# Stick-breaking attention with queries on partitions: suffix sums by a backwards scan on DVE

## The reference

```python
z = jnp.einsum('bqhd,bkhd->bhqk', qb, k).astype(jnp.float32) * scale
causal = key_pos[None, :] < t[:, None]
log_keep = jnp.where(causal, jax.nn.log_sigmoid(-z), 0.0)
suffix = lax.cumsum(log_keep, axis=3, reverse=True) - log_keep
attn = jnp.where(causal, jnp.exp(jax.nn.log_sigmoid(z) + suffix), 0.0)
return jnp.einsum('bhqk,bkhd->bqhd', attn, v.astype(jnp.float32)).astype(q.dtype)
```

## Time and profile before

| | |
|---|---|
| median of 3 runs | 2167.89 us (2167.81 to 2168.23) |
| the profiled execution: span from the first to the last instruction | 2165.9 us |
| PE busy with matmuls | 2142.8 us, 99% of the span |
| DVE busy | 1273.9 us, 59% |
| ACT busy | 784.7 us, 36% |
| PE's share of the chain that ended last | 95% |

### The profile page before, as it was taken

One profiled execution on the slowest core, in us unless ns is written; L12 is line 12 of the kernel. 1 busy time (PEld: TensorE's weight loads), 2 busy tenths in 40 slices (PEclk: granted clock), 3 DMA queues, 4 the chain that ended last, 5 costly groups with the idle time before them and its releaser, 6 DMA issues.

```text
span 2165.9 us, 24997 instructions
## 1 busy us (share of the span) xinstructions
PE 2142.8 (99%) x10363; PEld 1768.0 (82%) x10363; DVE 1273.9 (59%) x1673; ACT 784.7 (36%) x1044; POOL 26.6 (1%) x41
## 2 busy tenths in 40 slices
PE   7999999999999999999999999999999999999998
PEld 4888888888888887888888888888788888888887
DVE  6899897944665848435665554234843576555423
ACT  3323232323343354344343333135434435333312
POOL 1000000000000100000000000000000000000000
PEclk9999999999999999999999999999999999999999
DMA  9432232332232222312223232222232222323322
GB/s 316 145 117 83 97 103 83 99 115 98 98 102 98 98 79 78 131 64 92 84 86 110 82 113 97 88 77 88 78 124 71 85 91 80 113 81 111 103 88 78
DMA packets 181588, 217.86 MB, mean 101 GB/s; under 512 B 3932, under 2 KB 153188, under 8 KB 181220
## 3 DMA queue, kind: packets, MB, share of 16 engines
q1 hardware_dynamic: 178080, 209.47, 29.1%
q10 hardware_dynamic: 2948, 4.65, 0.6%
q0 software_dynamic: 448, 2.15, 0.3%
HBM read 212.06 MB, written 4.19 MB: 100 GB/s over the span
## 4 chain that ended last, share of the span: by engine, by line
PE 95%; DVE 2%; issue 1%; ACT 1%; DMA 0%; POOL 0%; SPq 0%; POOLq 0%; ACTq 0%; DVEq 0%
PE psum L1819 30%; PE psum L1821 30%; PE psum L1820 30%; PE psum L2234 1%; PE psum L2266 1%; DVE whl L518 1%; PE psum L1962 1%; PE psum L2246 1%; PE psum L2200 1%; DMA ada<-in_w_ada 0%; PE psum L2187 0%; PE psum L2219 0%; PE psum L1843 0%; POOL stat L682 0%; DVE hT L1502 0%
## 5 line engine op out<-in xcount | busy, mean ns | idle before, releaser
L1819 PE MATMUL psum<-hT,whl 128*128 128x512 f32 (+1 forms) x2064 | 789.4, 382 | 2.7 <-DVE whl L518 1.5
L1821 PE MATMUL psum<-hT,whl 128*128 128x512 f32 (+1 forms) x2064 | 783.3, 380 | 0.0
L1820 PE MATMUL psum<-hT,whl 128*128 128x512 f32 (+1 forms) x2064 | 783.1, 379 | 0.0
L518 DVE TENSOR_TENSOR whl<-raw,whl 128x1024 fp32r<-128x1024 f32 x361 | 438.5, 1217 | 429.2 <-ACT whl L511 428.9
L511 ACT ACTIVATE whl<-raw 128x1024 fp32r<-128x1024 f32 x361 | 376.7, 1047 | 421.5 <-PE psum L1821 387.1
L1819 PEld LDWEIGHTS psum<-hT,whl 128*128 128x128 f32 x2064 | 388.3, 188 | 84.2 <-issue 8.4
L1821 PEld LDWEIGHTS psum<-hT,whl 128*128 128x128 f32 x2064 | 388.3, 188 | 73.9
L1820 PEld LDWEIGHTS psum<-hT,whl 128*128 128x128 f32 x2064 | 388.4, 188 | 71.5 <-issue 0.2
L1819 PE MATMUL psum<-whl,ff 128*128 128x512 f32 x352 | 137.1, 390 | 0.0
L1821 PE MATMUL psum<-whl,ff 128*128 128x512 f32 x352 | 137.0, 389 | 0.0
L1820 PE MATMUL psum<-whl,ff 128*128 128x512 f32 x352 | 137.0, 389 | 0.0
(11 more groups left out here) (328 smaller groups left out, 2161.1 us busy)
## 6 DMA issues: line engine op xcount, KB each, us to landing
raw<-in_w_in SPq DMA_DIRECT2D x87, 1024.0 KB, 5.1
raw<-in_w_up SPq DMA_DIRECT2D x44, 1024.0 KB, 5.0
raw<-in_w_down SPq DMA_DIRECT2D x20, 1024.0 KB, 5.0
raw<-in_w_branch SPq DMA_DIRECT2D x12, 1024.0 KB, 5.1
raw<-in_w_out SPq DMA_DIRECT2D x12, 1024.0 KB, 5.0
ada<-in_w_ada SPq DMA_DIRECT2D x8, 1024.0 KB, 9.4
ada<-in_w_ada SPq DMA_DIRECT2D x8, 512.0 KB, 10.9
x<-in_x SPq DMA_DIRECT2D x4, 512.0 KB, 5.2
```

Source lines behind the costliest of these rows:

```text
L518: nc.vector.tensor_tensor(whl_view(w, 1), raw_view(w), whl_view(w, 0).bitcast(F), ALU.subtract).then_inc(w_lo, 1)
L1819: M(out_, stat_hi, mov_hi, start=start, stop=False, **kw)
L1820: M(out_, stat_hi, mov_lo, start=False, stop=False, **kw)
L1821: return M(out_, stat_lo, mov_hi, start=False, stop=stop, **kw)
```

## The change

Queries go on partitions and keys on columns, so that the sum over keys runs along the columns, and DVE does it by a scan.

- `sb_scores` exchanges the two operands, with the same segment widths, and adds the mask (eight `identb` times `sbaddb` matmuls) before it signals each head. The mask matrix is transposed.
- ACT's `sb_logs` stays. DVE's `sb_exponent(h)` at ph 1 and 2 takes the place of `sb_softplus` (ph 0, 1) and `sb_lo` (ph 2, 3): softplus, four scans that run backwards over a segment (`[:, ::-1]`), and z minus the running sum.
- ACT's `sb_exp` at ph 2 and 3 takes the exponential from SBUF to SBUF. PE's `sb_transposes(h)` at ph 4 and 5 takes the place of `sb_exponents`: ten 128x128 transposes to the head's banks. ACT's `sb_attnT` copies them to `sba`, and `sb_values` is as before.
- The split parts, `sbt`, `negtri`, `negones_r` and `sbmul` go, with their two copies on DVE at the start of the layers.

```diff
@@ ACT @@
-                def sb_hi(h):
-                    act.wait_ge(sp_ready, 2 * (4 * l + h) + 2)
-                    A(sphi[h % 2][:], sbs[h % 2][:], ACT.Copy).then_inc(sp_hi, 1)
-                    act.wait_ge(sp_sum, 4 * l + h + 1)
-                    A(sbt_hi[h % 2][:], sbt[h % 2][:], ACT.Copy).then_inc(sp_hi, 1)
-
                 def sb_exp(h):
+                    act.wait_ge(sb_e, 4 * l + h + 1)
+                    A(sbl[h % 2][:], sbs[h % 2][:], ACT.Exp).then_inc(sb_attn, 1)
+
+                def sb_attnT(h):
                     e = h % 2
-                    act.wait_ge(e_ps, 4 * l + h + 1)
+                    act.wait_ge(aT_ps, 4 * l + h + 1)
                     if h >= 2:
                         act.wait_ge(sbo_ps, 2 * l + h // 2)
-                    A(sba[e][:], psum[:, Z_BANK[e] * SEQ:Z_BANK[e] * SEQ + 1280], ACT.Exp).then_inc(sb_attn, 1)
+                    A(sba[e][:], psum[:, Z_BANK[e] * SEQ:Z_BANK[e] * SEQ + 1280], ACT.Copy).then_inc(aT_ready, 1)
...
-                        if ph in (1, 2):
-                            sb_hi(2 * p + ph - 1)
+                        if ph in (2, 3):
+                            sb_exp(2 * p + ph - 2)
                         if ph in (4, 5):
-                            sb_exp(2 * p + ph - 4)
+                            sb_attnT(2 * p + ph - 4)
@@ DVE @@
-                def sb_softplus(h):
+                def sb_exponent(h):
 
                     e = h % 2
+                    z = psum[:, Z_BANK[e] * SEQ:Z_BANK[e] * SEQ + 1280]
                     dve.wait_ge(sb_l, 4 * l + h + 1)
-                    link(V.scalar_tensor_tensor(sbs[e][:], psum[:, Z_BANK[e] * SEQ:Z_BANK[e] * SEQ + 1280], 0.0, sbl[e][:], ALU.max, ALU.add))
...
+                    link(V.scalar_tensor_tensor(sbs[e][:], z, 0.0, sbl[e][:], ALU.max, ALU.add))
+                    for b in range(TB):
+                        sp = sbs[e][:, SBO[3 - b]:SBO[3 - b] + SBW[3 - b]][:, ::-1]
+                        step(V.tensor_tensor_scan(sbl[e][:, SBO[3 - b]:SBO[3 - b] + SBW[3 - b]][:, ::-1], sp, sp, 0.0, ALU.add, ALU.max))
+                    dve.wait_ge(dve_chain, chain[0])
+                    V.scalar_tensor_tensor(sbs[e][:], sbl[e][:], -1.0, z, ALU.mult, ALU.add).then_inc(sb_e, 1)
...
-                        if ph in (2, 3):
-                            sb_lo(2 * p + ph - 2)
-                        if ph in (0, 1):
-                            sb_softplus(2 * p + ph)
+                        if ph in (1, 2):
+                            sb_exponent(2 * p + ph - 1)
@@ PE @@
-                    for kb in (0, 1, 3, 2):
+                    for b in (3, 2, 0, 1):
                         for e in range(2):
                             rows = slice(e * HEAD, (e + 1) * HEAD)
...
+                            M(psum[:, c0:c0 + SBW[3 - b]], sbq[rows, p, b * P:(b + 1) * P], sbk[rows, p, 0:(b + 1) * P],
+                              start=b != 0, stop=False, skip_group_check=True)
+                    for e in range(2):
+                        for b in range(TB):
+                            c0 = Z_BANK[e] * SEQ + SBO[3 - b] + b * P
+                            ins = M(psum[:, c0:c0 + P], identb[:], sbaddb[:], start=False, stop=True, skip_group_check=True)
+                        ins.then_inc(z_ps, 1)
+
+                def sb_transposes(h):
...
-                    pe.wait_ge(sp_lo, 4 * l + h + 1)
+                    pe.wait_ge(sb_attn, 4 * l + h + 1)
                     for kb in range(TB):
...
+                        for b in range(kb, TB):
+                            c0 = Z_BANK[e] * SEQ + SBO[kb] + (b - kb) * P
+                            a0 = SBO[3 - b] + kb * P
+                            ins = nc.tensor.transpose(psum[:, c0:c0 + P], sbl[e][:, a0:a0 + P], ident)
+                    ins.then_inc(aT_ps, 1)
                     for b in range(Z_BANK[e], Z_BANK[e] + 3):
-                        give(b, sb_attn, 4 * l + h + 1)
+                        give(b, aT_ready, 4 * l + h + 1)
```

More of the change, by code:

```diff
@@ L61 @@
 AV, AG, BB, BC, BH, BG, CA, CB, CG, MG = (8 * i for i in range(10))
-CONSTS = [("ident", 128), ("negtri", 128), ("sbmul", 128), ("corr", 64), ("sel", 256),
+CONSTS = [("ident", 128), ("corr", 64), ("sel", 256),
           ("freq", 1), ("sign", 1), ("mask", 512), ("sbadd", 128)]
@@ L83, in shape_constants @@
     put("ident", np.eye(P))
-    put("negtri", -(i[:, None] >= i[None, :]).astype(np.float32))
-    put("sbmul", (i[:, None] < i[None, :]).astype(np.float32))
-    put("sbadd", np.where(i[:, None] < i[None, :], 0.0, MASK))
+    put("sbadd", np.where(i[None, :] < i[:, None], 0.0, MASK))
     t = np.arange(16)
@@ L246, in build @@
     cst = keep("cst", [P, NKEEP])
-    tri_at = at[0]
     onesd = keep("onesd", [P, P])
@@ L260, in build @@
     assert at[0] <= top, at[0] - top
-    negtri_r = nc.alloc_sbuf_tensor_at("negtri_r", [P, P], R, offset=tri_at)
-    negones_r = nc.alloc_sbuf_tensor_at("negones_r", [P, P], R, offset=vcol_at)
     sel_r = nc.alloc_sbuf_tensor_at("sel_r", [P, 2, P], R, offset=cst_at + 4 * COFF["sel"])
@@ L334, in build @@
     sbs = [over(f"sbs{e}", (sb_at[e] + 5) * K, [P, 1280]) for e in range(2)]
[L335 to L339, removed]
     sba = [over(f"sba{e}", (sb_at[e] + 10) * K, [P, 1280]) for e in range(2)]
@@ L353, in build @@
     ident = cst[:, COFF["ident"]:COFF["ident"] + P]
-    negtri = cst[:, COFF["negtri"]:COFF["negtri"] + P]
-    sbmul = cst[:, COFF["sbmul"]:COFF["sbmul"] + P]
     freq = cst[:, COFF["freq"]:COFF["freq"] + 1]
@@ L404, in build @@
         row_full, row_read, s_ln, s_rt, s_sin, s_pos, s_tab = (sem(n) for n in ("row_full", "row_read", "lnrow_in", "rot_steps", "sines", "pos_in", "tables_ready"))
-        sp_hi, sp_lo = sem("sp_hi"), sem("sp_lo")
         hc_sum, sq_sum = sem("hc_summed"), sem("squares_summed")
-        rope_done, z_ps, sb_l, sp_ready, sp_sum, e_ps, sb_attn, sbo_ps, ob_hi, ob_lo = (
-            sem(n) for n in ("rope_done", "z_psum", "sb_log", "sp_ready", "sp_summed", "e_psum", "sb_attn",
+        rope_done, z_ps, sb_l, sb_e, sb_attn, aT_ps, aT_ready, sbo_ps, ob_hi, ob_lo = (
+            sem(n) for n in ("rope_done", "z_psum", "sb_log", "sb_exponent", "sb_attn", "attnT_psum", "attnT_ready",
                              "sbo_psum", "ob_hi", "ob_lo"))
@@ L1612, in _ @@
                 if l == 0:
-                    link(V.tensor_copy(negtri_r[:], negtri))
-                    step(V.tensor_copy(negones_r[:], negones[:]))
                     step(V.tensor_copy(sel_r[:], sel))
@@ L2192, in sb_exponents @@
-                def sb_exponents(h):
+                            c0 = Z_BANK[e] * SEQ + SBO[3 - b]
+                            M(psum[:, c0:c0 + SBW[3 - b]], sbq[rows, p, b * P:(b + 1) * P], sbk[rows, p, 0:(b + 1) * P],
[5 more added lines that the diff above has]
+                        ins.then_inc(z_ps, 1)
@@ L2194, in sb_exponents @@
+                def sb_transposes(h):
                     e = h % 2
-                    pe.wait_ge(sp_lo, 4 * l + h + 1)
+                    pe.wait_ge(sb_attn, 4 * l + h + 1)
                     for kb in range(TB):
[L2197 to L2204, removed]
-                        ins = M(psum[:, c0:c0 + P], identb[:], sbaddb[:], start=False, stop=True, skip_group_check=True)
@@ L2214, in sb_values @@
                         await_read(pe, ("sv", l, 1))
-                    pe.wait_ge(sb_attn, 4 * l + 2 * p + 2)
+                    pe.wait_ge(aT_ready, 4 * l + 2 * p + 2)
                     for kb in range(TB):
@@ L2309, in _ @@
                         if ph in (4, 5):
-                            sb_exponents(2 * p + ph - 4)
+                            sb_transposes(2 * p + ph - 4)
                         if ph == 6:
```

2 lines of the change are left out of this document (removed).

## The result

The changed kernel takes 2176.42 us (median of 4 runs, 2175.60 to 2177.34) against 2167.92 for the kernel before: ratio 1.004, interval 1.0028 to 1.0052, so it is 8.5 us slower. 2170.9 was forecast, with 2175.0 as the upper end. The profiled execution took 2177.34 us, with a span of 2175.5.

The account below looks back on a forecast made before the run. PE was taken to bound the kernel, unless DVE falls behind at two places. Per layer -1.07 + 3.77 - 1.19 = +1.51 us, for both layers +3.0: 2167.9 + 3.0 = 2170.9 us, range 2164.5 to 2175.0.

Parts of the forecast that it names:

- DVE's chain starts: First pair: DVE subtracts the next weight piece at 801.06, then runs without a gap to the end of sb_out.
- S: DVE's time for one head's four scans (512, 384, 256, 128 columns), priced like a strided addition: 2.94 us.
- rival 1: The scan spends two column times per column: S = 3.26, 2173.5 us; chance 0.33, with anything up to S = 4.
- second scores start: PE's scores of the second head pair, which overwrite bank 2 after DVE's last reading: at 834.8 + 2S, 840.68.
- second quarter starts behind them: First dvw tile's second quarter on PE writes bank 1, free after ACT's last qraw copy: Z + 31.93.
- Z: The moment at which the second pair's scores start on PE; DVE starts again at Z + 7.57.
- the two chains: DVE's work up to sb_out's end (second scores) and up to the rotation before ACT's last qraw copy (bank 1).
- The first wait: PE waits 0.8 us at the second pair's scores for DVE's last reading of bank 2.
- the sum: Both places less the fourth head's transposes: 4S - 10.25 us per layer, +1.51 at S = 2.94, +3.0 for both layers.
- (26.05 + 2S - 28.16): How much later than before PE starts the second quarter, once bank 1 is free: +3.77 us per layer.
- The rivals: Scan at two column times (0.33), like any DVE pass (0.20), like RECIPROCAL (0.02), or PE's work alone (nothing).
- The signs that were to show the forecast right: 512-column scan near 1.1 us, S near 2.9, transposes 1.2 per head, PE waits under 1.5 and 4 to 5 us.

Follow-up runs that it names:

- the kernel with the filled wait: The changed kernel with 32 useless matmuls on PE ahead of tile 12's matmuls, where PE would wait: 2171.69 us, ratio 1.0019.
- the kernel with four additions: The kernel before with four useless additions on DVE ahead of the rotation that ACT's last qraw copy needs: 2172.95 us, ratio 1.0026.
- the plain-pass kernel: The changed kernel with each head's four scans replaced by plain maxima over the same backward views, suffix sums left out: 2164.79 us, ratio 0.9987.

## Why the prediction was wrong

By its steps, layer 1:

| step | predicted | measured |
|---|---|---|
| DVE's chain starts | 801.06 | 801.13 |
| S, four scans | 2.94 (rival 1: 3.26) | 3.01 |
| second scores start | 840.68 | 841.06 |
| second quarter starts behind them | Z + 31.93 | Z + 32.07 |
| PE's wait there | 4.4 | 4.77 |
| eight mask matmuls | 0.55 | 0.43 |
| ten transposes | 1.21 | 1.01 |
| three quarters behind the wait | as before (4.09) | 6.98 |

**The places were right, and the scan's price too, in part by luck.** PE waits where the two chains end, each for the predicted releaser's work. Two slips of the working (801.06 + 33.68 is 834.74, not 834.8; 25.31 + 0.10 + 0.60 is 26.01, not 26.05) put 0.1 us too much on a layer, which changes nothing. The first wait came out as 1.65 us, not 0.8: 0.38 because DVE's end was later, the rest because PE was there earlier. The strided addition gave a good price for the scan, 2.94 us against 3.01. That is luck in so far as its two parts made up for each other: a column costs 2.03 ns (1.86 taken), and what is fixed is (3.01 - 1280 x 0.00203) / 4 = 0.10 us for each scan (0.14 taken). Against 1.055 ns for a plain column 2.03 is a factor of 1.92, so rival 1's price of a column (2.11 ns) was the nearest; its S came out too high mostly by the fixed part. Why a column costs that, no run shows. The half throughput that the Trainium skill states for the built-in scan ("DVE: opcode table, instruction layouts, handler registers and perf-mode slots", section "Datapath and trigger behaviour") agrees with this factor. The maximum over 512 columns, held against rival 1, was no guide to a scan.

**The step that failed is the sum.** Its term (26.05 + 2S - 28.16) prices the second wait at its length, 3.8 us net, and lets PE go on behind it as before. What followed was a stretch at half the clock, which the sum has no term for: 2.9 us in layer 1 and 7.08 - 4.09 = 3.0 in layer 2. The rest of the sum holds: -0.70 + 3.91 - 1.39 = +1.82 us per layer against a forecast of +1.51. With the missing 5.9 us it would have been 2167.9 + 3.6 + 5.9 = 2177.4, the profiled execution's own time; the others lie up to 1.7 us lower. The rivals put other prices on the scan or took the waits away; none had the clock, so the range could not hold it. The signs that were to show the forecast right came near or true (the first wait was 1.65 us, not under 1.5), but none of them looked at the matmuls behind a wait.

**The trace of before had a row for it.** The prediction set the first loads apart and went on. But PE's longest wait, 10.1 us, is followed by six matmuls of L1962, and the groups by form for 12.9 to 18.2 us and for 19.4 to 23 us (columns as in the earlier trace rows) show what they cost there and what the same form costs a little later:

```profile
L1962 PE MATMUL psum<-ada,stat 128*1 128x512 f32 x6 | 5.3, 1053 | 10.1 <-DMA ada<-in_w_ada 10.1
...
L1962 PE MATMUL psum<-ada,stat 128*1 128x512 f32 x8 | 3.6, 592 | 0.0
```

Six take 0.88 us each, eight 0.45: half the speed behind the wait. The granted clock's column reads 1.00 in both stretches, so the start of this program shows the slow matmuls by their durations alone, and that it is the clock there too isn't shown. It was reason enough for a rival that prices the wait and a slow stretch behind it. The Trainium skill has the rule as well ("TensorE: Matmul & The Clock Gate", section "HAM oscillation — how this bites in real kernels"): a kernel that leaves the array idle between bursts pays part of the next burst at half rate. This case's traces agree, with 2.9 us behind 4.77.

**The chances.** Within 0.2% had 0.57, and the time is 0.4% up. Slower than that had 0.35, but for a scan of more than 3.11 us, and the scan took 3.01. Without the fall of the clock the change would have cost +3.6 us, inside 0.2%; in the kernel with the filled wait, which takes the fall away and leaves most else, it is +4.0 (2171.69 against 2167.7).

## What to carry over

Where a sum opens a wait of several us on a PE that never waited, price it twice: once for its length, and once for the matmuls behind it at half the clock (here 1.6 us behind 2.23, and 2.4 to 3.0 behind 4.8). Look behind the longest waits that the trace already has for what the next matmuls cost. Where such a wait hangs on one engine's chain, look first for idle time at that chain's start: here it was 10 us on DVE, behind ACT passes in an order that could be changed, and with that reordering the same edit turned from 0.4% slower to 0.4% faster.

## What the runs showed of the hardware

- The clock fell to 0.50 behind waits of 4.77, 4.78 and 4.80 us, and (0.51 from 873.10 on) behind one of 3.43. Behind 1.65 and 1.91 us it stayed at 1.00 in the profiled executions. About 2.2 us both happened: 2.23 with a fall, 2.25 without. Executions in steps of some 1.6 us, in the kernel with four additions and, less clearly, in the plain-pass kernel, would fit a fall that comes or not; only one execution of each was profiled, so this is not shown.
- With 3.43 and 2.23 us of waiting the first matmuls behind the wait still ran 0.23 to 0.34 us apart, and only then came the slow ones. The first matmul behind a wait therefore doesn't tell.
- A scan on DVE costs 2.03 ns per column, 1.9 times a plain pass, and running backwards costs nothing that shows (1.73 us for four plain instructions over 1280 columns, where the common rate gives 1.9).
